# Input transposed raw, kept in DRAM and added by VectorE after the output product; first products in between the transposes

## The reference

```python
h = jnp.concatenate([meta_b, x], axis=1)          # 16 + 1024 tokens
xn = rms_norm(h, norm1_g)
p = xn @ w_in                                     # c_lat, k_idx, w_idx, q_idx, u_pool, q, ... are columns of p
...
m = g[:, :, 0] * y_a + g[:, :, 1] * y_b + g[:, :, 2] * y_c
h = h + m @ w_o                                   # the residual is the input, not normed
hn = rms_norm(h, norm2_g)
gate, up = jnp.split(hn @ w_gate_up, 2, axis=-1)
return h + (jax.nn.silu(gate) * up) @ w_down
```

## Time and profile before

| | before |
|---|---|
| runs | 2384.61, 2386.1, 2389.65 us, median 2386.1 |
| profiled execution | 2385.08 us, its span 2383.3 us |
| TensorE | 2208.1 us busy, 93% of the span |
| VectorE, ScalarE, GpSimd busy | 58%, 38%, 42% |
| TensorE's mean granted clock | 0.969 |

### The profile page before, as it was taken

The page is one execution under the profiler, slowest core; times in us unless marked ns, Lnnn a source line. Parts: engine busy times, 40 slices in busy tenths (PEclk is TensorE's granted clock), DMA queues, the critical chain, the costliest instruction groups (busy, mean ns, idle before and its releaser), DMA issues.

```text
span 2383.3 us, 29803 instructions
## 1 busy us (share of the span) xinstructions
PE 2208.1 (93%) x10812; PEld 1819.3 (76%) x10812; DVE 1388.7 (58%) x2754; ACT 906.5 (38%) x1620; POOL 1003.3 (42%) x575
## 2 busy tenths in 40 slices
PE   6999999999999989999579999999999798998896
PEld 6876788998887777778458888888888576877874
DVE  3268899999613667550556666665467526307723
ACT  5244422322235744322322332233455333226732
POOL 1355333555442332233365555545579523120042
PEclk9999999999999999999789999999999799999998
DMA  3122111111242121250224444446855121110212
GB/s 108 52 62 67 49 49 53 45 46 48 76 141 80 54 80 41 89 181 27 88 71 169 137 168 137 168 155 221 316 175 172 53 106 37 53 45 15 88 41 88
DMA packets 232948, 229.48 MB, mean 96 GB/s; under 512 B 9825, under 2 KB 177406, under 8 KB 232814
## 3 DMA queue, kind: packets, MB, share of 16 engines
q1 hardware_dynamic: 228822, 214.56, 27.8%
q10 hardware_dynamic: 3992, 13.11, 1.4%
HBM read 169.82 MB, written 56.89 MB: 95 GB/s over the span
## 4 chain that ended last, share of the span: by engine, by line
PE 70%; DVE 9%; POOL 3%; ACT 3%; issue 3%; DMA 1%; SPq 0%; ACTq 0%; DVEq 0%
PE ps L876 22%; PE ps L1128 17%; PE ps L1150 9%; PE ps L1193 8%; PE ps L1011 6%; PE ps L1339 3%; PE ps L1043 1%; POOL xl_P L2761 1%; DVE logit L2038 1%; PE ps L986 1%; PE ps L1029 1%; ACT p_s L1865 1%; PE ps L1077 1%; DVE pt_lo L2057 1%; POOL x_lo L2848 1%
## 5 line engine op out<-in xcount | busy, mean ns | idle before, releaser
L2570 POOL TENSOR_TENSOR w_lo<-w_raw,w_hi 128x1024 fp32r<-128x1024 f32 (+1 forms) x135 | 290.8, 2155 | 896.7 <-ACT w_hi L1371 896.7
L876 PE MATMUL ps<-x_hi,w_hi 128*128 128x512 f32 (+2 forms) x1008 | 379.7, 377 | 7.7 <-DVE c_rs L1956 3.3
L876 PE MATMUL ps<-x_lo,w_hi 128*128 128x512 f32 (+2 forms) x1008 | 375.9, 373 | 0.0
L876 PE MATMUL ps<-x_hi,w_lo 128*128 128x512 f32 (+2 forms) x1008 | 374.0, 371 | 0.0
L1128 PE MATMUL ps<-xh_P,wr_hi 128*128 128x512 f32 x616 | 246.8, 401 | 36.7 <-issue 21.9
L1128 PE MATMUL ps<-xl_P,wr_hi 128*128 128x512 f32 x616 | 245.7, 399 | 0.0
L1128 PE MATMUL ps<-xh_P,wr_lo 128*128 128x512 f32 x616 | 245.6, 399 | 0.0
L876 PEld LDWEIGHTS ps<-x_hi,w_hi 128*128 128x128 f32 x1008 | 191.3, 190 | 44.0 <-issue 8.4
L876 PEld LDWEIGHTS ps<-x_hi,w_lo 128*128 128x128 f32 x1008 | 191.4, 190 | 29.0
L876 PEld LDWEIGHTS ps<-x_lo,w_hi 128*128 128x128 f32 x1008 | 191.3, 190 | 27.8
L2013 DVE MATCH_REPLACE8 score<-best,score 128x400 f32<-128x400 f32 (+3 forms) x224 | 185.0, 827 | 0.0
(11 more groups left out here) (394 smaller groups left out, 4773.0 us busy)
## 6 DMA issues: line engine op xcount, KB each, us to landing
...
```

The costliest lines, as they stand in the source:

```text
L876: mm = pe.matmul(ps[:, b, 0:n], w[:, s, P * k:P * k + P], r[:, k, t0:t0 + n], start=k == 0 and i == 0, stop=k == kd - 1 and i == 2 and ext ...
L2570: pool.tensor_tensor(w_lo[:, p % 2, 0:n], w_raw[:, p % 2, 0:n], w_hi[:, p % 2, 0:n], ALU.subtract).then_inc(wlo_done, 1)
```

## The change

The input's tiles are transposed twice. First unscaled: TensorE turns all nine `x_tok` tiles into PSUM, VectorE (12 chunks) and ScalarE (4, and the 16 meta tokens) copy them to `xt_f`, and SyncE stores that to `xt_scratch` in DRAM. Then scaled, as before, but through banks 4 to 7. The first tile of `c` and of `kw` is multiplied once the first group of tokens is split, with the transposes of the other groups between its matmuls. The ten small loads go to ScalarE's queue. At the output product the matmuls against the identity and `x_res` are gone: SyncE loads the transposed input tile by tile into a ring `xtr` of four, and VectorE adds it as it empties the bank. The stores to `h_scratch` go out panel by panel, and the load of the second gate and up pair stands behind them.

```diff
-    panel(("kw", 0), 3)
+    panels += [("c", 0), ("kw", 0)]
+    tiles += [(("c", 0), 0), (("kw", 0), 0), (("c", 0), 1), (("c", 0), 2), (("kw", 0), 1), (("kw", 0), 2)]
     for m in range(2):
         panel(("qi", m), 2)
...
@@ -414,6 +415,7 @@
 
         x_load = [sem(f"x_load{r}") for r in range(9)]
         vec_load, const_ready, vec_full, vec_ready = sem("vec_load"), sem("const_ready"), sem("vec_full"), sem("vec_ready")
...
-            for name, row in VEC.items():
-                n = int(np.prod(I[name].shape)) // P
-                a = I[name]
-                a = a.rearrange("(n p) -> n p", p=P) if len(a.shape) == 1 else (
-                    a[0].rearrange("(n p) -> n p", p=P) if len(a.shape) == 2 else a[0].rearrange("t (n p) -> (t n) p", p=P))
-                sp.dma_start(vec_rows[row:row + n, :], a).then_inc(vec_load, 16)
-
...
+            def load_residual(n):
+                if n >= 4:
+                    sp.wait_ge(h_done, n - 3)
+                m, h = n // 2, n % 2
+                sp.dma_start(xtr[:, n % 4, :], xt_scratch[m][:, META + BANK * h:META + BANK * h + BANK]).then_inc(xt_load[n % 4], 16)
+
...
+                if key == ("qi", 0):
+                    sp.wait_ge(xr_dve, 12)
+                    sp.wait_ge(xr_act, 5)
+                    for c in range(KD):
+                        sp.dma_start(xt_scratch[c], xt_f[:, c, :]).then_inc(xts_store, 16)
...
-                    sp.dma_start(x_res[:, :, :], x.rearrange("(r p) d -> p r d", p=P)).then_inc(xres_load, 16)
+                    for n in range(4):
+                        load_residual(n)
+                if kind == "wo" and m >= 4:
+                    load_residual(2 * m - 4)
+                    load_residual(2 * m - 3)
...
-            sp.wait_ge(h_done, 2 * KD)
+            for m in range(KD):
+                if m < 4:
+                    load_residual(12 + m)
+                sp.wait_ge(h_done, 2 * m + 2)
+                sp.dma_start(h_scratch[m], mix[:, m, :]).then_inc(hs_store, 16)
             load_pair(1)
-            for m in range(KD):
-                sp.dma_start(h_scratch[m], mix[:, m, :]).then_inc(hs_store, 16)
...
+            def raw_turn(g):
+
+                for r in XGROUPS[g][1]:
+                    pe.wait_ge(x_load[r], 32 if r == 0 else 16)
+                    for c in range(KD):
+                        if r == 0 and c == KD - 1:
+                            pe.wait_ge(vec_ready, 1)
+                        if r == 4:
+                            pe.wait_ge(xr_dve, c + 1)
+                        mm = pe.transpose(ps[:, c, P * (r % 4):P * (r % 4) + P], x_tok[:, r, P * c:P * c + P], ident[:, :])
+                        if r % 4 == 3:
+                            mm.then_inc(xr_full, 1)
+
+            raw_turn(0)
+            raw_turn(1)
+            pe.wait_ge(x_load[8], 16)
+            pe.wait_ge(xr_act, 4)
+            for c in range(KD):
+                mm = pe.transpose(ps[:, 3, META * c:META * c + META], x_tok[0:META, 8, P * c:P * c + P], ident[0:META, 0:META])
+            mm.then_inc(xr_full, 1)
+
+            def turned(n):
+                t0, tiles, w = XGROUPS[n // KD]
+                c = n % KD
                 pe.wait_ge(xs_done, tiles[-1] + 1)
-                for c in range(KD):
-                    if n >= 4:
-                        pe.wait_ge(xlo_done, n - 3)
-                    for r in tiles:
-                        k = tile_rows(r)
-                        mm = pe.transpose(ps[:, n % 4, P * (r % 4):P * (r % 4) + k], x_tok[0:k, r, P * c:P * c + P], ident[0:k, 0:k])
-                    mm.then_inc(xt_full, 1)
-                    n += 1
-            pe.wait_ge(xlo_done, 24)
-            product(("c", 0), x_hi, x_lo, FULL)
-            product(("kw", 0), x_hi, x_lo, FULL)
+                if n >= 4:
+                    pe.wait_ge(xlo_done, n - 3)
+                else:
+                    pe.wait_ge(xr_dve, KD + n + 1)
+                for r in tiles:
+                    k = tile_rows(r)
+                    mm = pe.transpose(ps[:, 4 + n % 4, P * (r % 4):P * (r % 4) + k], x_tok[0:k, r, P * c:P * c + P], ident[0:k, 0:k])
+                mm.then_inc(xt_full, 1)
+
+            def first_tile(kind, j, group, between=None):
+                p = PANEL_AT[kind, 0]
+                pe.wait_ge(wlo_done, p + 1)
+                pe.wait_ge(xlo_done, KD * group + KD)
+                b, (t0, n) = open_tile(TILE_AT[(kind, 0), j]), FULL[j]
+                for k in range(KD):
+                    for i, (w, r) in enumerate(((w_hi, x_hi), (w_hi, x_lo), (w_lo, x_hi))):
+                        mm = pe.matmul(ps[:, b, 0:n], w[:, p % 2, P * k:P * k + P], r[:, k, t0:t0 + n],
+                                       start=k == 0 and i == 0, stop=k == KD - 1 and i == 2)
+                    if k == KD - 1:
+                        mm.then_inc(lin_full, 1)
+                    if between is not None:
+                        between(k)
+
+            for n in range(12):
+                turned(n)
+            first_tile("c", 0, 0, lambda k: turned(12 + k // 2) if k % 2 else None)
+            first_tile("kw", 0, 0, lambda k: turned(16 + k))
+            first_tile("c", 1, 1)
+            first_tile("c", 2, 2)
+            first_tile("kw", 1, 2)
+            first_tile("kw", 2, 2)
             for m in range(2):
...
-            pe.wait_ge(xres_load, 16)
             for m in range(KD):
-                def residual(j, b, m=m):
-                    for r in range(4):
-                        mm = pe.matmul(ps[:, b, P * r:P * r + P], x_res[:, 4 * j + r, P * m:P * m + P], ident[:, :],
-                                       start=False, stop=r == 3)
-                    return mm
-                product(("wo", m), x_hi, x_lo, HALF, extra=residual, ready=mlo_done if m == 0 else None)
+                product(("wo", m), x_hi, x_lo, HALF, ready=mlo_done if m == 0 else None)
...
+            act.wait_ge(vec_full, 1)
+            act.copy(vec[:, :], ps[:, 7, 0:rows]).then_inc(vec_ready, 1)
...
                 for r in tiles:
-                    k = tile_rows(r)
-                    act.wait_ge(x_load[r], 32 if r == 0 else 16)
-                    if r >= 2:
-                        act.wait_ge(sq_done, r - 1)
-                    act.activation(junk[0:k, r % 2, :], x_tok[0:k, r, :], ACT.Square, accum_out=ss[0:k, r:r + 1]).then_inc(sq_done, 1)
+                    squared(r)
+                if gi == 1:
+                    for c in range(4):
+                        act.wait_ge(xr_full, KD + c + 1)
+                        act.copy(xt_f[:, c, BANK:2 * BANK], ps[:, c, :]).then_inc(xr_act, 1)
                 k = tile_rows(tiles[0])
                 act.wait_ge(inv_done, gi + 1)
                 act.activation(rstd[0:k, tiles[0]:tiles[-1] + 1], rstd[0:k, tiles[0]:tiles[-1] + 1], ACT.Sqrt).then_inc(rt_done, 1)
+            act.wait_ge(xr_full, 2 * KD + 1)
+            act.copy(xt_f[:, :, 2 * BANK:T], ps[:, 3, 0:P].rearrange("p (c t) -> p c t", t=META)).then_inc(xr_act, 1)
             split(0)
             split(1)
-            act.wait_ge(vec_full, 1)
-            act.copy(vec[:, :], ps[:, 7, 0:rows]).then_inc(vec_ready, 1)
             act.wait_ge(vec_ready, 1)
...
-                for j, (t0, w) in enumerate(HALF):
-                    b = tile(("wo", m), j)
-                    act.copy(mix[:, m, t0:t0 + w], ps[:, b, :]).then_inc(h_done, 1)
...
+                for c in ((range(KD), range(4, KD), ())[gi]):
+                    dve.wait_ge(xr_full, KD * gi + c + 1)
+                    dve.tensor_copy(xt_f[:, c, t0:t0 + w], ps[:, c, :]).then_inc(xr_dve, 1)
...
+                dve.wait_ge(xr_full, KD * gi + KD if gi < 2 else 2 * KD + 1)
                 for r in tiles:
                     dve.tensor_scalar(x_tok[0:k, r, :], x_tok[0:k, r, :], rstd[0:k, r:r + 1], None, ALU.mult).then_inc(xs_done, 1)
...
-            combined_weights(0)
+            for m in range(KD):
+                for j in range(2):
+                    n = 2 * m + j
+                    dve.wait_ge(xt_load[n % 4], XT_LOAD_0[n % 4] + 16 * (n // 4 + 1))
+                    dve.wait_ge(lin_full, TILE_AT[("wo", m), j] + 1)
+                    dve.tensor_tensor(mix[:, m, half(j)], ps[:, bank(("wo", m), j), :], xtr[:, n % 4, :], ALU.add).then_inc(h_done, 1)
+                if m == KD - 3:
+                    combined_weights(0)
             for q in range(SLOTS):
                 block_low(q)
```

35 lines of the change are left out of this document (25 added, 10 removed).

## The result

The changed kernel takes **2367.5 us** (median of 4 runs, 2365.16 to 2370.91), the kernel before 2385.36 in the same comparison: a ratio of 0.9923, 95% interval 0.9903 to 0.9942. Its profiled execution took 2365.47 us, 19.6 less than that of before. The prediction was 2364.5, between 2357 and 2374.

A forecast was written before the change was run, and what follows sets the result against it. TensorE was taken to bound the kernel, 70% of the chain. Start 4.1 more, output product 20.1 less, behind the last tile 5.1 less: -21.1 us from 2385.1, 2364.0 profiled; forecast 2364.5, between 2357 and 2374.

The forecast's parts named there:

- Output product, 20.1 us: Identity matmuls removed, 14.2 us, plus waits and slow clock ahead of the output product gone, 5.9 us: 20.1 us less.
- the queue: At the border of `wb1` and `wo`: without the 4 MB of `x_res` queued ahead of `g1h`, 5.9 us go.
- Rival D: Output product: `xtr` loads land so late that TensorE waits for the additions; slower than before, 2389 us, chance 0.03.
- One of my signs: Sign that the prediction is right, ahead of the output product: `gy_s` waits under 3 us.
- Behind the last tile, 5.1 us: After the output product: scaling of `mix` no longer waits for stores, 6.2 us gained, 1.1 added before the norm: 5.1 less.
- `block_low`: Three of them between the last addition and `n_acc` add 2.1 us, 1.1 covered by a gap; 1.1 with a longer eviction.
- The start, 4.1 us: From the beginning to the last `kw` tile: read at 64.7 instead of 60.60, 4.1 us more.
- Steps (3) to (6): Start: VectorE's copies end near 17.8, ScalarE's squares and copies by 25, VectorE's scaling until 29.5, `x_lo` near 32.5.
- (1): Start: ten small-load issues on ScalarE end near 4.2; the gains are there near 7.7, and the squares start then.
- (8): Start: 16 large and 8 small transposes between matmuls add 2.8 us; last `kw` tile at 62.4 at best, 67 at worst.
- (7): Start: first product needs eight `x_lo` steps, not 24, and starts 2 to 3 us later than 35.95; transposes end 38 to 39.
- From the last `kw` tile to gate 13, zero: Up to the third last `gy_s`: same program, so the start's shift passes through with nothing gained or lost.

The follow-up runs named there:

- residual_side_alone: The changed kernel's residual side on the start of the kernel before, adding the input untransposed, so another output; 2357.19 us, ratio 0.9875.
- small_loads_behind: The changed kernel with the ten small loads issued by SyncE behind the input again, as before the change; 2376.29 us.
- small_loads_first: The changed kernel with the ten small loads issued by SyncE ahead of the input; 2372.06 us.
- meta_rows_at_once: The kernel `raw_kept` with the eight small transposes of the last 16 rows behind one another; 2356.52 us, ratio 0.9878.
- raw_kept: The changed kernel with scaled rows in their own place, seven raw half tiles turned ahead, ten between products, squares and `block_low` earlier; 2360.63 us, ratio 0.9888.
- gains_behind_tile_2: The changed kernel with the gains transposed behind the raw blocks of tiles 0 to 2, and squares of tiles 0 to 3 ahead of their copy; 2366.13 us.
- block_low_ahead: The changed kernel with the three `block_low` ahead of the last panel's additions; 2364.75 us.

## Why the prediction was right, and where its sizes were off

**Output product, 20.1 us: right.** 20.2 measured from gate 13 to the last squares, and both parts apart: 6.1 for the queue (5.9 predicted), 14.1 left for the identity matmuls (14.2). The sixteen additions are 11.0 us on VectorE, 0.69 each, as taken from `gy_s`, and TensorE never waits for them:

```profile
L2225 DVE TENSOR_TENSOR mix<-ps,xtr 128x512 f32<-128x512 f32 x16 | 11.0, 690 | 62.7 <-PE ps L889 62.7
```

The idle time ahead of them is all VectorE's wait for TensorE. Rival D needed the opposite. One of my signs isn't met: `gy_s` waits 3.95 us for its gate and not under 3. That wait costs nothing, since TensorE is busy throughout. The 14 us and the queue's 6 are one edit's two effects, and neither page nor diff shows the second; only the timeline did.

**Behind the last tile, 5.1 us: right in sum, by two errors.** 5.3 measured. The stores are 5.9 (6.2 predicted); `block_low` added 0.6 to `n_acc`, not 1.1. Moving it gave 2.2, of which 0.6 are its own and 1.6 TensorE's clock in the sums; in the kernel before these were at 1.2 GHz as well (3.57 us for the sixteen), so my term is to be set against the 0.6. That both kernels met the same level there is luck: `residual_side_alone`, with the changed kernel's work, gains 6.4 over the same stretch. Behind the scaling 1.3 us more were gained by the first down product and 1.0 after it; I had zero, and what gave them wasn't traced.

**The start, 4.1 us: the size was off, 6.4 measured.** Steps (3) to (6) came out nearly as written (`x_lo` at 32.80 for 32.5), by errors that met: (1) the small loads landed at 9.78, where I had TensorE begin at 7.4, so the copies began at 14.56 for 12.9, and what was behind them took less than I had given it. Against the three other kernels with the unedited start it is 4.9 to 6.1. The step that was mis-sized is (8): "Between its matmuls stand 16 large and 8 small transposes, 2.8 us at the faster level". Six tiles without anything between them take 0.48 for a step of three matmuls. This is the end of `kw`'s first tile in the changed kernel:

```profile
50.75 0.43 PE L945 MATMUL ps<-x_hi,w_hi 128*128 128x352 f32 x1
...
51.42 0.23 PE L935 MATMUL ps<-ident,x_tok 16*128 16x16 f32 x1
51.58 0.43 PE L945 MATMUL ps<-x_hi,w_hi 128*128 128x352 f32 x1
...
52.17 0.32 PE L945 MATMUL ps<-x_hi,w_hi 128*128 128x352 f32 x1
...
52.65 0.33 PE L945 MATMUL ps<-x_hi,w_hi 128*128 128x352 f32 x1
```

A step with a small transpose takes 0.83 (50.75 to 51.58), one without 0.48 (52.17 to 52.65). I had counted the transposes' own time alone; a step with one costs 0.35 more, though eight behind one another take 0.64 together (at 26.19, above). The rest goes with the change from one kind to the other and back: in `meta_rows_at_once` eight interruptions made one take 2.1 us less. The two interleaved tiles take 39.26 to 51.58, 12.32 us, against 16 steps of 0.48, 7.7: **4.6 us for 2.8**. The eight small transposes are 2.8 of them; the sixteen large ones, in four groups, are 1.8 and about their own time.

The low end of (8), 62.4, was a first product at 37 and the clock up through the tiles. The clock was up (1.00 from 40 to 50), the first product came at 39.26 (38 to 39 by (7)), 2.3 later than 37, and the transposes cost 1.8 more: 66.5 of the 67.01. So the 67 at the upper end was reached, but not by the stretch at 1.2 GHz that I had kept it for.

On the small loads the Trainium skill's "DMA: Bandwidth & Descriptors" was read in two ways in the prediction. By its section "Queues, rings and completion order" they land early, and 9.78 against 16.60 on SyncE's queue behind the input agrees. Its section "Issuing engines are not separate DMA queues" has the transfers of all engines interleave on the same 16 DMA engines, and only issue time saved by a second engine. What I read into that, that the loads would end with the input, isn't what happened; `small_loads_behind` shows what it costs here, 6.5 us at the last `kw` tile. Still they need 4.7 us from the last issue's end (5.08) beside the input's transfers, where `small_loads_first` has 1.1 (4.20 to 5.29) with nothing issued ahead of them.

**From the last `kw` tile to gate 13, zero: wrong by 1.8 us.** I said that the shift passes through whole. The work is the same, but the clock isn't, and 1.8 is only what these two profiles met. Windows of TensorE (busy us, granted clock, DMA), first of the kernel before:

```profile
120.00:140.00 20.00, 16.83 (x126) 1.00 0.15 42
140.00:160.00 20.00, 20.00 (x136) 1.00 0.16 53
```

and of the changed kernel:

```profile
120.00:140.00 20.00, 18.49 (x127) 1.00 0.19 53
140.00:160.00 20.00, 18.36 (x119) 0.91 0.10 27
```

Behind TensorE's idle time around the score's first step (135.6 before, 141.2 now) the changed kernel works at a mean of 0.91, the kernel before at 1.00: 0.09 of 20 us is 1.8, and the shift grows by 1.5 from that step (+5.6) to the first store of `q` (+7.1). Two profiles of the kernel before give the same windows there to 0.01 us, and each kernel with another shift has other ones (`raw_kept` 0.91 and 1.00, `gains_behind_tile_2` 0.92 and 0.91). Nor does it take a shift of microseconds. `block_low_ahead`, with the same program up to there and 0.3 us ahead of the changed kernel, has another level a little later. First the changed kernel, then this one:

```profile
260.00:280.00 20.00, 16.04 (x72) 0.83 0.16 52
```

```profile
260.00:280.00 20.00, 15.56 (x75) 0.91 0.16 52
```

With this and a window near 900 (0.97 against 1.00 from 900 to 950) it is 3.3 us ahead at gate 13, and its shift fell by 1.3 where the changed kernel's grew by 1.8. So stages with idle time in them can cost or gain one or two microseconds each, in an amount that I can't forecast; why the levels fall as they do wasn't found.

**Sum by what was measured:** 6.4 + 1.8 - 20.2 - 5.3 - 2.3 = -19.6, against -21.1 on record. The profiled execution lies 2.0 below the median of its kernel and I had allowed 0.5 for that, which makes the rest of the 3.0 us by which 2364.5 was short. That the total came this near is luck in part: 4.1 us of loss that I hadn't seen up to gate 13 met 2.6 of gain that I hadn't seen behind it.
